# Gate projections moved from the joint input windows into the first mixers of pairs, other window bounds, a quarter-size last inversion level, and key norms from keys times keys

## The chip, the cores and the metric

The kernel runs on one NeuronCore of one Trainium2 chip. The time is the device time of one launch in microseconds (us).

## The reference, cut to what matters

One decoder layer on x of 1024 tokens by 1024 features, float32. Two mixers (retention and gated delta rule) share one input projection; then every token takes 8 x 16 experts out of 16384 by product keys, and each expert is a row of `peer_u` and a row of `peer_v`.

```python
h = _rmsnorm(x, ln1_w[l]); proj = (h @ w_in[l])
rq, rk, rv, rg, gq, gk, gv, gz, ga, gb = jnp.split(proj, offsets, axis=-1)
o_r = groupnorm(_retention(rope(rq), rope(rk), rv))
y_r = o_r * ret_norm_w[l] * jax.nn.silu(rg)
cq, ck, cv = split(silu(causal_conv(concat([gq, gk, gv]))))
q_g = cq * lax.rsqrt(jnp.sum(cq * cq, -1) + NORM_EPS)
k_g = ck * lax.rsqrt(jnp.sum(ck * ck, -1) + NORM_EPS)
o_g = _gated_delta_rule(q_g, k_g, cv, g_dec, beta)   # per chunk: m = I + strict(beta k k^T decay), a 128x128 triangular solve
y_g = _rmsnorm(o_g, gdn_norm_w[l]) * jax.nn.silu(gz)
x = x + concat([y_r, y_g]) @ w_out[l]
h2 = _rmsnorm(x, ln2_w[l])
# _peer: q = h2 @ wq; top-16 of each half; top-16 of the sums -> ids, gate
act = gelu(einsum('tkd,td->tk', u_tab[ids], h2))
x = x + einsum('tk,tkd->td', gate * act, v_tab[ids]); return _rmsnorm(x, lnf_w)
```

## The kernel before, in words

The 1024 tokens are eight chunks of 128. All engines run their own instruction lists, written out in Python and joined by semaphores.

**The expert stream.** Chunk n has 64 steps (PAIRS), 512 in all. A step is two gathers on GpSimd's queue (L452), each of 128 rows of 8 KB (u and v of one expert), 1.05 MB. VectorE takes the dot product of the u half with the token (L1161), ScalarE makes gelu and a diagonal tile (L841, L847), TensorE multiplies the diagonal by the v half into `y_ps` (L476). The ten `uv` buffers (RING) hold five steps: the gather of step s waits until TensorE has done step s-5 (`v_used`). Each engine has its own `upto(place)`, which deals it the steps up to that place between other work; TensorE deals step s-1 where the others deal s.

**Windows and mixers.** `window(n)` gives two places in the stream (numbers of steps). Inside window n, `route` of chunk n runs: the last two query products, scores, the top-16 on VectorE in groups of heads (`GROUPS`), which end in `ids` (L1519), and, if chunk n+1 is "alone" or "first", `inputs(n+1)`: norm, transposes, input projections. Between window n and window n+1 lies the mixer of chunk n+1 (`mix`), whose 34 marks (`turn`) are spread by the table PIECES. KIND is start, alone, then (first, second) three times: for a pair, `inputs` of the first chunk projects both chunks from the same weight block, one product for `actT` and one for `actT_ahead`. So windows 1, 3 and 5 hold joint projections of chunks (2, 3), (4, 5), (6, 7); windows 2, 4, 6, 7 hold none. I call mixers 2, 4, 6 first mixers, and 3, 5, 7 second mixers.

**Weights.** A projection of 512 columns (IN_NAMES: gk, gq, gv, rqk, rv, rg, gz) is two blocks of 1 MB. SyncE loads them one after the other (L410) into two buffers `wbuf`, each when the block two before it is used up (`consumed`). Per `inputs` there are 14 blocks, per chunk 4 for the output and 8 for the queries.

**Banks.** Everything else that TensorE makes goes round six PSUM banks in the order of the list `USES`; `take` waits until the use six before has been read.

**The inverse.** The mixer inverts the 128x128 matrix of each of 4 heads in levels T1, 1 to 6. Level i: P = NT x T, masked by VectorE into Pm, then Q = TT x Pm and R = Pm x TT, subtracted from T and TT (L709 to L716, L1361 to L1369). The norms of q and k come from squares (L993) and eight products with ones (L655); `kk` is made late, from k and k times beta (`kbT`, L1269), and NT is `kk` times the decay mask.

**The start.** Chunk 0 has no stream beside it; between its marks TensorE makes late products (`FILL`, L555). ScalarE issues four constant loads (L915) right after `hT`.

## Time and profile before

| what | value |
|---|---|
| median of three runs | 3143.29 us |
| lowest, highest | 3141.07, 3143.57 us |
| the profiled execution's own time | 3143.25 us |
| its span | 3141.3 us (1.95 us less) |
| busy: TensorE, VectorE, ScalarE, GpSimd | 76%, 66%, 37%, 37% |
| moved by DMA | 1265.78 MB, 403 GB/s over the span |

How to read it: no engine is busy all the time, and the DMA engines are. The profile gives the moved GB/s of each stretch; a stretch that falls below the rate of the others is one in which data were not asked for in time. Traces are cut here at the places where the windows begin and end (the dot product of that step on VectorE).

### The profile page before, as it was taken

What the parts mean: (1) busy time and instruction counts of PE and PEld (TensorE: products, weight loads), DVE (VectorE), ACT (ScalarE), POOL (GpSimd) and SP (SyncE); (2) the same over time, 40 slices, a digit from 0 to 9 for tenths busy, and PEclk for the clock granted to TensorE, in tenths of its full rate; (3) what the DMA queues carried; (4) which work ended last, traced back from release to release, by engine and by line L of the source; (5) the groups of instructions that cost most, each with busy time, mean ns of one, the idle gap of its engine ahead of it and who ended that gap; (6) DMA issues with size and microseconds to landing.
All of it is one profiled execution on the core that took longest, in us unless ns stands there. A gap on an engine that the chain in (4) does not pass through costs nothing.

```text
span 3141.3 us, 36341 instructions
## 1 busy us (share of the span) xinstructions
PE 2386.6 (76%) x12496; PEld 1389.6 (44%) x12496; DVE 2076.6 (66%) x5408; ACT 1173.6 (37%) x3421; POOL 1175.5 (37%) x1030
## 2 busy tenths in 40 slices
PE   8877787998874787997876587798787567765554
PEld 7753355764541345663552144575355124431111
DVE  4475855668579854667749874656856976486444
ACT  2233433344334432435323533424433343232222
POOL 0033533235333442334434443234443444344442
PEclk9998898998987898998998789899998689877777
DMA  8399999999999999999999999999999999999997
GB/s 344 141 405 420 417 411 401 396 409 419 420 415 400 419 420 420 386 418 419 419 420 415 420 419 416 390 405 420 419 420 420 420 419 418 419 402 418 420 420 319
DMA packets 177736, 1265.78 MB, mean 403 GB/s; under 512 B 21520, under 2 KB 21776, under 8 KB 25104
## 3 DMA queue, kind: packets, MB, share of 16 engines
q0 software_dynamic: 147456, 1073.81, 83.0%
q1 hardware_dynamic: 28368, 183.72, 14.2%
q10 hardware_dynamic: 1728, 5.94, 0.5%
q8 instruction: 99, 1.62, 0.2%
q14 instruction: 85, 0.70, 0.1%
HBM read 1259.19 MB, written 4.19 MB: 402 GB/s over the span
## 4 chain that ended last, share of the span: by engine, by line
DMA 36%; PE 36%; DVE 16%; ACT 6%; issue 3%; POOL 3%; SPq 0%; ACTq 0%; POOLq 0%; DVEq 0%
DMA uv<-uv_tab,ids 33%; PE y_ps L476 13%; PE bank L533 8%; DVE uv L1161 7%; PE bank L525 7%; PE bank L540 3%; POOL uv L452 3%; DMA wbuf<-w 2%; ACT diag L847 2%; PE y_ps L555 1%; DVE area L1221 1%; DVE area L1455 1%; PE bank L590 1%; DMA uv<-w 1%; ACT gelu L841 1%
## 5 line engine op out<-in xcount | busy, mean ns | idle before, releaser
L452 POOL DMA_INDIRECT uv<-uv_tab,ids x1024 | 1175.0, 1147 | 1933.0 <-PE y_ps L476 1589.8
L1161 DVE CUSTOM_DVE_ANT_0 uv<-uv,h 128x1024 f32<-128x1024 f32 x1024 | 1237.6, 1223 | 783.9 <-DMA uv<-uv_tab,ids 777.4
L476 PE MATMUL y_ps<-uv,diag 128*64 128x512 f32 x4096 | 1187.2, 712 | 515.2 <-ACT diag L847 494.1
L476 PEld LDWEIGHTS y_ps<-uv,diag 128*64 128x64 f32 x4096 | 289.1, 156 | 1168.5 <-ACT diag L847 687.4
L841 ACT ACTIVATE gelu<-dots 128x2 f32<-128x2 f32 x512 | 104.1, 203 | 1429.8 <-DVE dots L1161 1429.4
L533 PE MATMUL bank<-actT,wbuf 128*128 128x128 f32 x2688 | 343.0, 289 | 42.8 <-DMA wbuf<-w 37.8
L533 PEld LDWEIGHTS bank<-actT,wbuf 128*128 128x128 f32 x2688 | 329.6, 204 | 99.8 <-issue 72.4
L847 ACT ACTIVATE diag<-gated,gelu 128x64 f32<-128x64 f32 x1024 | 300.7, 340 | 66.9 <-PE y_ps L476 8.2
L837 ACT ACTIVATE gated<-smalls,gate 128x64 f32<-128x64 f32 x1024 | 293.9, 336 | 7.8 <-DVE acc L1175 7.8
L525 PE MATMUL bank<-wbuf,actT 128*128 128x256 f32 x960 | 226.8, 390 | 23.3 <-DMA wbuf<-w 21.5
L525 PEld LDWEIGHTS bank<-wbuf,actT 128*128 128x128 f32 x960 | 181.7, 194 | 91.7 <-issue 49.5
L540 PEld LDWEIGHTS bank<-arena 128*128 128x128 f32 x1208 | 150.6, 199 | 78.6 <-issue 57.2
L540 PE MATMUL bank<-arena 128*128 128x128 f32 x1208 | 167.2, 291 | 10.9 <-DVE arena L1361 9.0
L841 ACT ACT_TABLE_LOAD x90 | 115.5, 1283 | 1.6
L1455 DVE FIND_INDEX8 area<-area,arena 128x8 uint32<-128x128 f32 (+1 forms) x384 | 99.9, 279 | 0.0
L590 PE MATMUL bank<-keys_sb,arena 128*128 128x128 f32 x256 | 44.3, 327 | 69.5 <-ACT arena L869 68.5
L525 PE MATMUL bank<-wbuf,actT_ahead 128*128 128x256 f32 x384 | 89.1, 385 | 0.0
L1451 DVE MAX8 area<-arena 128x8 f32<-128x128 f32 (+1 forms) x384 | 79.8, 273 | 9.6 <-ACT arena L1081 4.6
L1221 DVE SCALAR_TENSOR_TENSOR area<-conv_in,conv_w,area 128x128 f32<-128x128 f32 x288 | 82.1, 347 | 2.5
L1161 DVE DVE_READ_ACCUMULATOR2_ANT dots<- 128x1 f32 x1024 | 83.7, 82 | 0.0
L525 PEld LDWEIGHTS bank<-wbuf,actT_ahead 128*128 128x128 f32 x384 | 71.1, 190 | 26.6 <-issue 17.8
L590 PEld LDWEIGHTS bank<-keys_sb,arena 128*128 128x128 f32 x256 | 37.6, 226 | 84.4 <-ACT arena L869 71.2
(221 smaller groups left out, 1874.2 us busy)
## 6 DMA issues: line engine op xcount, KB each, us to landing
wbuf<-w SPq DMA_DIRECT2D x146, 1024.0 KB, 9.5
uv<-w SPq DMA_DIRECT2D x20, 1024.0 KB, 23.9
uv<-uv_tab,ids POOLq DMA_INDIRECT x1024, 16.1
acc<-x SPq DMA_DIRECT2D x8, 512.0 KB, 12.8
y<-acc ACTq DMA_DIRECT2D x8, 512.0 KB, 7.6
rowbuf<-x SPq DMA_DIRECT2D x5, 512.0 KB, 12.6
actT_ahead<-x SPq DMA_DIRECT2D x3, 512.0 KB, 19.1
keys_sb<-keysT ACTq DMA_DIRECT2D x1, 1024.0 KB, 16.0
```

The source lines that it names most:

```text
L452: nc.gpsimd.indirect_dma_start(out=uv[i % RING][:, :, :].rearrange("p z d -> p (z d)"), out_offset=None, in_=uv_tab, in_offset=bass.Indire ...
L476: done = mm(y_ps[z][64 * j:64 * j + 64, :], diag[:, i % DIAGS, :], uv[i % RING][:, 1, 512 * z:512 * z + 512], start=(s % PAIRS == 0), stop ...
L525: last = mm(b[:, WB * half_:WB * half_ + WB], src[:, k, :], wb[:, k, :], start=(k == 0), stop=(k == KT - 1))
L533: last = mm(b[:, o:o + P], wb[:, k, P * i:P * i + P], src[:, k, :], start=(k == 0), stop=(k == KT - 1))
L540: last = mm(b[:, P * h:P * h + P], lhs[:, h, :], rhs[:, h, :], start=True, stop=True)
L590: last = mm(b[:, P * i:P * i + P], qT[:, t, :], keys_sb[:, t, :], start=True, stop=True)
L837: made = A(gated[:, step % 2, j, :], stack, ACT.Copy, scale=gate[n % 2][:, j, pair:pair + 1])
L841: A(gelu[:, step % 2, :], dots[:, d0:d0 + 2], ACT.Gelu).then_inc(S["gelu"], 1)
L847: made = A(diag[:, (2 * step + j) % DIAGS, :], gated[:, step % 2, j, :], ACT.Copy, scale=gelu[:, step % 2, j:j + 1])
L1161: V.tensor_tensor_reduce(out=u, in0=u, in1=h2[n % 2][:, j, :], scale=1.0, scalar=0.0, op0=ALU.mult, op1=ALU.add, accum_out=dots[:, i % DOT ...
L1221: last = V.scalar_tensor_tensor(dst, src, conv_w[:, i, j:j + 1], dst, ALU.mult, ALU.add)
L1455: last = V.max_index(index(t)[:, o:o + 8], vals(t)[:, o:o + 8], src(t))
```

## The change

Windows: joint ones become longer (34 steps instead of 30), the second mixers shorter. The four gate blocks (rg, gz) of a pair leave `inputs` and are made in the first mixer, eight matmuls at each of the marks 6 to 13, both chunks into halves of one bank. The last level makes only the one 64x64 quarter of P and R that is not zero, and no Q. `kk` comes early from k times k; its diagonal gives the squares for k's norm on VectorE (`kk_sums`); the beta row now multiplies the decay mask. At the start the four constant loads are issued later. Chunks 4, 6 and 7 get three groups of heads instead of two. What is computed is the same.

| window n | 1 | 2 | 3 | 4 | 5 | 6 | 7 |
|---|---|---|---|---|---|---|---|
| before | 55 to 83 | 118 to 138 | 176 to 206 | 244 to 264 | 304 to 334 | 372 to 392 | 436 to 456 |
| after | 55 to 82 | 119 to 140 | 172 to 206 | 246 to 267 | 300 to 334 | 374 to 395 | 438 to 458 |

```diff
-GROUPS = [[(0, 1), (1, 2), (2, 4), (4, PH)] if n == 0 else [(0, 2), (2, 4), (4, PH)] if n < 3 else [(0, 3), (3, PH)]
+GROUPS = [[(0, 1), (1, 2), (2, 4), (4, PH)] if n == 0 else [(0, 2), (2, 4), (4, PH)] if n in (1, 2, 4, 6, 7) else [(0, 3), (3, PH)]
...
-        for name, event in zip(LATE_NAMES, LATE_EVENTS):
+        for name, event in zip(LATE_NAMES[0:2 if kind == "first" else 4], LATE_EVENTS):
             uses += projection(name, event)
-    uses += own(("gc", "gc_in", 1, 0), ("gc_row", "E", 1, 0), ("ss", "norm_in", 1, 0),
-                ("kT", "kst", 1, 0), ("qk", "attn", 1, 0), ("beta_row", "kbT", 1, 0),
-                ("vT", "vb", 1, 0), ("kk", "NT", 1, 0),
-                ("T1", "inv_TT", LEVELS, 0))
+    uses += own(("gc", "gc_in", 1, 0), ("gc_row", "E", 1, 0), ("kk", "NT", 1, 0), ("ss", "norm_in", 1, 0),
+                ("kT", "kst", 1, 0), ("qk", "attn", 1, 0), ("beta_row", "NT", 1, 0),
+                ("vT", "vb", 1, 0), *gates("rg0"),
+                ("T1", "inv_TT", LEVELS, 0), *gates("rg1"))
     for i in range(1, LEVELS):
-        uses += level(i)
+        uses += level(i) + own(*gates({1: "gz0", 2: "gz1"}.get(i)))
...
+GATE_FILL = {mark: 8 for mark in range(6, 14)}
+GATED = [p + 0.75 * (i in GATE_FILL) for i, p in enumerate(PIECES)]
-WINDOW = {"first": (16, 14), "second": (12, 8), None: (12, 8)}
+WINDOW = {"first": (20, 14), "second": (10, 11), None: (10, 10)}
-        return ((-3, 22), (55, 83), (118, 138))[n]
+        return ((-3, 22), (55, 82), (119, 140))[n]
...
+            def gates_late(c):
+                n = c.n
+                for name in ("rg0", "rg1", "gz0", "gz1"):
+                    b = take(n, name)
+                    wb = weight_block()
+                    for a, src in enumerate((actT, actT_ahead)):
+                        for k in range(KT):
+                            last = mm(b[:, WB * a:WB * a + WB], src[:, k, :], wb[:, k, :], start=(k == 0), stop=(k == KT - 1))
+                            if k == KT - 1 and a:
+                                last.then_inc(gates_made, 1)
+                            yield
...
             def inputs(c, at):
-                names = IN_NAMES[0:3] if c.kind == "start" else IN_NAMES
+                names = IN_NAMES[0:{"start": 3, "first": 5}.get(c.kind, 7)]
-                at(0.22 if n < 2 else 0.26)
+                early = 0 if n < 2 else 7 / length(n - 1)
+                at(early or 0.22)
-                first = 0.25 if n < 2 else 0.29
+                first = 0.25 if n < 2 else 8 / length(n - 1)
-                products, done = 14 * len(projected), [0]
+                products, done = 2 * len(names) * len(projected), [0]
...
                 all_rows(n, "gc_row", T[:, :, :])
+                pe.wait_ge(*event("silu_conv", n, 0))
+                by_head(n, "kk", conv[:, 4:8, :], conv[:, 4:8, :])
-                for i in range(2 * H):
+                for i in range(H):
                     last = mm(b[:, i:i + 1], norms[:, i, :], ones[:, 0:1], start=True, stop=True)
...
-                pe.wait_ge(*event("kbT", n))
-                by_head(n, "kk", conv[:, 4:8, :], kbT)
...
+                    if i == LEVELS - 1:
+                        b = take(n, f"P{i}")
+                        for h in range(H):
+                            last = mm(b[64:128, P * h:P * h + 64], NT[0:64, h, 64:128], T[0:64, h, 0:64], start=True, stop=True)
...
+                        b = take(n, f"R{i}")
+                        for h in range(H):
+                            last = mm(b[0:64, P * h + 64:P * h + 128], Pm[64:128, h, 0:64], TT[64:128, h, 64:128],
+                                      start=True, stop=True)
+                        continue
...
-                at(0.20 if n < 2 else 0.24)
+                at(0.20 if n < 2 else 6.3 / length(n - 1))
...
                 if n == 0:
-                    for dst, src in ((ret_qdec[:, :, :], qdec), (smalls[:, :], small),
-                                     (keys_sb[:, :, :], keysT), (lnf_row[:, :], rows.partition_broadcast(P))):
-                        act.dma_start(dst, src).then_inc(late_in, 16)
...
                 if c.kind == "start":
+                    for dst, src in ((ret_qdec[:, :, :], qdec), (smalls[:, :], small),
+                                     (keys_sb[:, :, :], keysT), (lnf_row[:, :], rows.partition_broadcast(P))):
+                        act.dma_start(dst, src).then_inc(late_in, 16)
                     return
...
+                    if c.kind == "first" and i == 1:
+                        follows(act, "ret_mixed", n)
+                        gates_block("rg0", gate_r, "gR_half")
...
+                    b = filled(dve, "kk", c)
+                    for h in range(H):
+                        last = V.tensor_tensor_reduce(out=NT[:, h, :], in0=b[:, P * h:P * h + P], in1=ident, scale=1.0, scalar=0.0,
+                                                      op0=ALU.mult, op1=ALU.add, accum_out=st[:, 88 + h:89 + h])
+                    last.then_inc(S["kk_sums"], 1)
...
-                V.tensor_tensor(kbT[:, :, :], conv[:, 4:8, :], heads(filled(dve, "beta_row", c)), ALU.mult
-                                ).then_inc(S["kbT"], 1)
+                link(V.tensor_tensor(kbT[:, :, :], cmask[:, :, :], heads(filled(dve, "beta_row", c)), ALU.mult))
-                V.tensor_tensor(NT[:, :, :], heads(filled(dve, "kk", c)), cmask[:, :, :], ALU.mult).then_inc(S["NT"], 1)
+                V.tensor_tensor(NT[:, :, :], heads(filled(dve, "kk", c)), kbT[:, :, :], ALU.mult).then_inc(S["NT"], 1)
...
-                early = 0.22 if n > 0 else 0.37
+                early = 5.9 / length(n) if n > 0 else 0.37
```

What moves, at the places of which the prediction speaks. TensorE in window 3, from the replication of the tokens (L790, after L860) on: transposes (L500, after L537), the small products for a and b (L615, L666), the projections (L533, L570) and the stream's steps (L476, L513; x4 is one step). Before:

```order
L476 MATMUL y_ps<-uv,diag 64x512 x12
L500 MATMUL bank<-tab,rowbuf 128x128 x8
L500 MATMUL bank<-tab,actT_ahead 128x128 x8
L476 MATMUL y_ps<-uv,diag 64x512 x4
L615 MATMUL bank<-w_ab_sb,actT 128x8 x8
L615 MATMUL bank<-w_ab_sb,actT_ahead 128x8 x8
L533 MATMUL bank<-actT,wbuf 128x128 x16
L476 MATMUL y_ps<-uv,diag 64x512 x4
L533 MATMUL bank<-actT_ahead,wbuf 128x128 x16
L476 MATMUL y_ps<-uv,diag 64x512 x4
L533 MATMUL bank<-actT,wbuf 128x128 x16
L533 MATMUL bank<-actT_ahead,wbuf 128x128 x16
```

After:

```order
L513 MATMUL y_ps<-uv,diag 64x512 x8
L537 MATMUL bank<-tab,rowbuf 128x128 x8
L537 MATMUL bank<-tab,actT_ahead 128x128 x8
L513 MATMUL y_ps<-uv,diag 64x512 x4
L666 MATMUL bank<-w_ab_sb,actT 128x8 x8
L666 MATMUL bank<-w_ab_sb,actT_ahead 128x8 x8
L570 MATMUL bank<-actT,wbuf 128x128 x16
L513 MATMUL y_ps<-uv,diag 64x512 x8
L570 MATMUL bank<-actT_ahead,wbuf 128x128 x16
L513 MATMUL y_ps<-uv,diag 64x512 x4
L570 MATMUL bank<-actT,wbuf 128x128 x16
L513 MATMUL y_ps<-uv,diag 64x512 x4
```

One step fewer lies ahead of the transposes, two follow the first projection, and from there on one or two steps stand between two projections, where before there were one or none.

TensorE in mixer 2, from the last step ahead of T1 to level 2. Before:

```order
L476 MATMUL y_ps<-uv,diag 64x512 x12
L500 MATMUL bank<-tab,arena 128x128 x4
L476 MATMUL y_ps<-uv,diag 64x512 x8
L540 MATMUL bank<-arena 128x128 x4
L500 MATMUL bank<-tab,area 128x128 x4
L476 MATMUL y_ps<-uv,diag 64x512 x4
L540 MATMUL bank<-arena 128x128 x8
L476 MATMUL y_ps<-uv,diag 64x512 x4
L540 MATMUL bank<-arena 128x128 x4
```

After (L630 is half of a gate block, eight matmuls of one chunk):

```order
L513 MATMUL y_ps<-uv,diag 64x512 x8
L630 MATMUL bank<-wbuf,actT_ahead 128x256 x8
L537 MATMUL bank<-tab,arena 128x128 x4
L513 MATMUL y_ps<-uv,diag 64x512 x8
L630 MATMUL bank<-wbuf,actT 128x256 x8
L577 MATMUL bank<-arena 128x128 x4
L537 MATMUL bank<-tab,area 128x128 x4
L513 MATMUL y_ps<-uv,diag 64x512 x8
L630 MATMUL bank<-wbuf,actT_ahead 128x256 x8
L577 MATMUL bank<-arena 128x128 x8
L513 MATMUL y_ps<-uv,diag 64x512 x4
L630 MATMUL bank<-wbuf,actT 128x256 x8
```

The gate products stand between the levels, each behind one or two steps.

VectorE in the mixer of chunk 0, between the decay rows and the reciprocal of the norms. Before:

```order
L1246 TENSOR_TENSOR st<-bank,st 128x4
L1219 TENSOR_SCALAR area<-conv_in,conv_w 128x128 x4
L1221 SCALAR_TENSOR_TENSOR area<-conv_in,conv_w,area 128x128 x12
L1224 COPY conv_in<-conv_in 128x4x3
L1258 RECIPROCAL st<-st 128x8
```

After (L1341 is the new sum over the diagonal):

```order
L1341 ISA arena,st<-bank,tab 128x128
L1341 ISA st 128x1
L1341 ISA arena,st<-bank,tab 128x128
L1341 ISA st 128x1
L1341 ISA arena,st<-bank,tab 128x128
L1341 ISA st 128x1
L1341 ISA arena,st<-bank,tab 128x128
L1341 ISA st 128x1
L1311 TENSOR_SCALAR area<-conv_in,conv_w 128x128 x4
L1313 SCALAR_TENSOR_TENSOR area<-conv_in,conv_w,area 128x128 x12
L1316 COPY conv_in<-conv_in 128x4x3
L1355 RECIPROCAL st<-st 128x8
```

The third convolution now stands behind four sums that wait for `kk`.

## Rows read from the trace of the kernel before

**Rows 1.** The page: busy time, DMA rate by slice, table loads, gathers.
```profile
PE 2386.6 (76%) x12496; PEld 1389.6 (44%) x12496; DVE 2076.6 (66%) x5408; ACT 1173.6 (37%) x3421; POOL 1175.5 (37%) x1030
...
GB/s 344 141 405 420 417 411 401 396 409 419 420 415 400 419 420 420 386 418 419 419 420 415 420 419 416 390 405 420 419 420 420 420 419 418 419 402 418 420 420 319
...
L841 ACT ACT_TABLE_LOAD x90 | 115.5, 1283 | 1.6
...
uv<-uv_tab,ids POOLq DMA_INDIRECT x1024, 16.1
```

**Rows 2.** By stage: busy PE, PEld, DVE, ACT, POOL; clock, DMA share, GB/s.
```profile
0.00:142.40 142.40, 123.75 (x874) 114.18 (x875) 63.20 (x215) 40.16 (x79) 5.29 (x11) 0.98 0.60 233
...
302.30:485.70 183.40, 143.10 (x750) 81.36 (x746) 126.79 (x282) 80.86 (x231) 73.90 (x64) 0.89 1.01 415
485.70:680.30 194.60, 176.14 (x1075) 127.82 (x1074) 126.03 (x397) 74.54 (x207) 59.39 (x54) 0.93 0.98 398
680.30:884.20 203.90, 163.21 (x841) 93.77 (x840) 132.77 (x290) 85.28 (x243) 83.51 (x74) 0.91 1.01 420
884.20:1003.90 119.70, 74.91 (x384) 36.37 (x383) 106.83 (x364) 43.19 (x124) 46.99 (x41) 0.82 0.98 403
1003.90:1209.60 205.70, 157.72 (x804) 88.95 (x805) 139.18 (x301) 87.52 (x256) 86.91 (x76) 0.88 1.01 420
1209.60:1412.50 202.90, 181.48 (x1090) 129.20 (x1091) 126.88 (x377) 75.47 (x214) 66.39 (x57) 0.93 0.99 406
...
1964.20:2165.80 201.60, 182.14 (x1094) 129.97 (x1094) 126.81 (x376) 76.15 (x214) 65.97 (x56) 0.93 0.98 402
...
2739.40:2853.90 114.50, 78.31 (x379) 36.22 (x380) 101.62 (x335) 41.12 (x122) 47.65 (x39) 0.77 1.00 407
```

**Rows 3.** The same columns, stretches of 10 us in window 1, then window 5.
```profile
540.00:550.00 10.00, 6.39 (x24) 3.49 (x24) 9.68 (x41) 8.27 (x22) 6.20 (x6) 0.53 0.73 277
...
570.00:580.00 10.00, 10.00 (x79) 8.09 (x79) 9.00 (x33) 4.68 (x12) 2.10 (x2) 1.00 0.96 362
...
650.00:660.00 10.00, 10.00 (x46) 6.54 (x42) 6.51 (x10) 4.19 (x12) 4.63 (x4) 1.00 0.88 337
...
2030.00:2040.00 10.00, 10.00 (x54) 8.71 (x53) 8.76 (x28) 5.53 (x18) 0.40 (x1) 0.66 0.69 285
2040.00:2050.00 10.00, 10.00 (x79) 8.29 (x78) 7.93 (x38) 0.86 (x3) 4.66 (x4) 1.00 0.69 237
```

**Rows 4.** Timeline, TensorE, window 5: start, us, line, shape, count, [idle before].
```profile
2002.40 2.08 PE L590 MATMUL bank<-keys_sb,arena 128*128 128x128 f32 x8 [12.07 <-ACT arena L869]
...
2031.94 6.48 PE L533 MATMUL bank<-actT,wbuf 128*128 128x128 f32 x32
2038.34 1.94 PE L476 MATMUL y_ps<-uv,diag 128*64 128x512 f32 x8
...
2049.52 3.74 PE L533 MATMUL bank<-actT_ahead,wbuf 128*128 128x128 f32 x32
```

**Rows 5.** Waits of the whole span: total us, times, longest.
```profile
POOL uv L452 <- DVE ids L1519: 144.7, 2, 135.2
...
ACT gate_g L869 <- PE bank L525: 35.1, 6, 8.0
```

**Rows 6.** Timeline, TensorE in mixer 5: an output block, shaped as a gate block.
```profile
1901.95 3.72 PE L525 MATMUL bank<-wbuf,actT 128*128 128x256 f32 x16
```

**Rows 7.** Timeline of the start, and from the page the landing of the keys.
```profile
41.25 3.57 PE L655 MATMUL bank<-tab,area 128*128 128x1 f32 x16 [3.15 <-ACT area L993]
...
45.31 0.20 DVE L1258 RECIPROCAL st<-st 128x8 f32<-128x8 f32 x1 [1.47 <-ACT st L978]
...
58.91 0.41 DVE L1298 TENSOR_TENSOR area<-qk_r,ropes 128x256 f32<-128x256 f32 x1
...
93.50 1.95 PE L540 MATMUL bank<-arena 128*128 128x128 f32 x16
...
keys_sb<-keysT ACTq DMA_DIRECT2D x1, 1024.0 KB, 16.0
```

104 lines of the change are left out of this document (82 added, 22 removed).

## The prediction

> **What bounds the kernel now.** I read the page first [rows 1]: TensorE is busy 76% and VectorE 66% of the span, while the rate in most slices is 419 to 420 GB/s. The full rate is the bound, and the change removes no transfer, so a gain can only come from time in which the DMA engines are short of requests. I call that time lost: length x (1 - GB/s / 420). The table by stage [rows 2] says where it is. The start loses 142.4 x (1 - 233/420) = 63.4 us. The windows with joint projections, 1, 3 and 5, lose 10.2, 6.8 and 8.6 us, 25.6 together. Windows 2 and 7 lose 4.8 and 3.5, mixer 1 loses 2.2, mixers 2 and 3 nothing.
>
> In windows 3 and 5 TensorE is busy 181.5 of 202.9 us and 182.1 of 201.6. But it isn't short of time evenly. The cut into 10 us [rows 3] shows 285 and 237 GB/s at 2030 to 2050: 3.2 + 4.4 = 7.6 of the 8.6 us of window 5. The timeline there [rows 4] tells why. TensorE waits 12.07 us for ScalarE's copy of the queries; then come replication, transposes, the small products, and a first projection of 6.48 us in a stretch whose granted clock is 0.66, between the levels of 1.2 and 2.4 GHz; at 1.00 a step takes 1.94 us and a projection 3.74. The ring holds 5 steps x 5.0 us (2 x 1.05 MB at 420 GB/s) = 25 us, of which a gather needs 16.1 to land [rows 1]: some 9 us are left for everything else, and this burst is longer. In window 1 the same burst comes after a stretch at 277 GB/s (3.4 us lost) [rows 3]: GpSimd waited for the ids, once at the start (135.2 us) and once for 144.7 - 135.2 = 9.5 us [rows 5]. Window 1 then stays short: 362 and 337 GB/s long after the burst [rows 3].
>
> **The change part by part.**
>
> *Pace of the joint projections.* One product of one chunk and one block takes 3.74 us [rows 4], call it 3.8. Before, windows 3 and 5 hold 28 of them in 0.71 x 30 = 21.3 steps: 1.31 x 3.8 + 1.94 = 6.9 us of TensorE per step. DMA needs 5.0 + 14/21.3 x 2.5 (a block of 1.05 MB) = 6.6. After, 20 in 26 steps: 0.77 x 3.8 + 1.94 = 4.9 against 5.0 + 10/26 x 2.5 = 6.0. Window 1: 7.3 against 6.8 before, and after, with 20 in 19 steps, 5.9 against 6.3. So TensorE is under DMA everywhere after the burst, with little room in window 1.
>
> *The burst.* By the order of the instructions the transposes come one step earlier after the replication (two steps ahead instead of three), so one step is held behind the first projection that was not, and its gather comes up to 10 us later. The steps after it come 3 to 6 us earlier, since no two projections stand together any more. I take 7.6 us down to about 5. The norm of x also no longer waits for VectorE's next step: the reciprocals stand 7.5 steps into the window in both, but the window has begun 4 steps sooner.
>
> Windows 3 and 5 together: from 15.4 to 9.4, **-6 us**. Bounds: all of it gone, -15; the burst 1 us worse each and nothing behind it to win, +2. Window 1: its ids come half a step earlier (62 instead of 62.5 dealt), which is worth 1 of the 3.4 us, and what lies behind the burst goes: 10.2 to 5.2, **-5 us** (bounds -9, 0).
>
> *Gate blocks in the first mixers.* Four blocks for two chunks are 8 x 3.72 us [rows 6] = 29.8 us of TensorE. Mixer 2 grows by 2 steps: TensorE 163.2 + 29.8 + 2 x 1.94 = 197 us, in 203.9 + 2 x 5.0 + 4 x 2.5 = 224 us: 88%, where the joint windows that lose are at 90%. The cover is TensorE's idle time between levels; its order puts a step ahead of each piece, and behind it the product P or Q of the level, for which VectorE waits up to 3.7/2 + 1.94 us longer. VectorE has 65% there. The two blocks for gz are loaded 3 marks ahead of their use, about 4 steps or 20 us. I take +0.5 us for each of three, **+1.5** (bounds -0.5 and +9; the upper is 3 us a mixer, what the burst costs a window of the same load).
>
> *Shorter second mixers.* Mixer 3 goes from 38 to 32 steps: 205.7 - 30 = 176 us for TensorE's 157.7 - 6 x 1.94 = 146 and VectorE's 139.2 - 6 x 2.6 = 124. The nearest row is mixer 1, 33 steps in 183.4 us, which loses 2.2 [rows 2]. Mixer 5 is alike (33 steps), mixer 7 hardly changes. **+1.5** (0 to +4).
>
> *Windows 2, 4, 6, 7.* 20 or 21 steps as before. The first group of two heads is ready 0.25 x 21 = 5.25 steps into a window that opens 2 steps later, where 3 heads were ready at 7.5: the same place within half a step. A third group adds some 5 us of VectorE: window 2, which has three, takes 106.8 us, window 7 with two 101.6 [rows 2]. Their losses, 4.8 and 3.5, show no order by groups. **0** (-3 to +4).
>
> *Last level and norms.* Away from the start they are hidden under DMA. At the start nothing hides them: TensorE is busy 123.8 of 142.4 us. Q and R of a level take 1.95 us [rows 7], P half of that; four products of 64 columns instead of 128 halve P and R, and Q goes: 2.9 to 1.0, -1.9 us. Eight products with ones go from the 3.57 us [rows 7], but `kk` and the sum stand in their place. VectorE reaches the reciprocal (45.31) only after the third convolution: about 3 us later; it waits 1.47 us there and about 2.5 us more behind it until T1, so I book +0.5. The four constant loads (1.7 MB, 4 us at full rate) leave the stretch of the first weight blocks; 4 us is the most that can give, and with TensorE busy for all but 18.6 us of the start I take 1.0. They are first needed at 58.91 [rows 7]; issued some 2 us ahead of the products with ones (41.25), with 16.0 us to land [rows 7], they are there at 55, if the last of the four isn't slower. Start: **-2.4** (-4 to +3).
>
> A rule of the Trainium skill bears on the last level: by "TensorE: Matmul & The Clock Gate" (Part 2: What happens when you issue a matmul) a product takes as many cycles as columns stream in, however few rows it has. A quarter of the area then costs half the time; by area it would be a quarter, and the start 0.5 us better. No row of before has a product of 64 columns.
>
> ScalarE gets 13 more table loads, 16.7 us at 1.283 us each [rows 1]; it is busy 37% of the span, and the row shows 1.6 us of idle time ahead of 90 loads. "ScalarE: Activation LUTs" of the Trainium skill (What ACT_TABLE_LOAD costs) adds a drain of 1.38 us to each, 35 us in all; no row here shows it, and the sum would not change.
>
> **The sum.** 3143.25 us, the profiled execution's own time (span 3141.3 and 1.95 around it, 0.04 below the median): -2.4 - 5 - 6 + 1.5 + 1.5 + 0 = -10.4, so **3133 us**.
>
> **The rivals.**
>
> *The burst is the whole loss.* Pace is not the cause; only what lies behind the bursts goes, about 2 us a window (in window 5: 8.6 - 7.6 = 1.0, in window 1 some 3). Then -2.4 - 6 + 3 = -5.4: 3138 us. For it: 7.6 of 8.6 us lie in 20 us. Against: the order behind the first projection changes too.
>
> *All joint loss goes.* The earlier norm and the slower pace lift both: -2.4 - 25.6 + 1 = -27: 3116 us. For it: a demand well under DMA's. Against: the 12.07 us wait and the half clock stay.
>
> *Slower: ScalarE is held by the gate blocks.* In its fixed order ScalarE waits for TensorE's product before it goes on with gelu and diagonals. Such waits were 35.1 us in 6, 5.9 each [rows 5]. The first mixers get 12. A wait costs nothing while the 9 us of the ring hold; beyond them, with VectorE's chain waiting for P in the same marks, each costs about 1.5 us: +18, and with the other terms 3133 - 1.5 + 18 = 3150 us. For it: TensorE at 88%. Against: mixer 2 lost nothing with ScalarE at 42%.
>
> *The start goes the wrong way.* Constants late, convolution in the path: +3 instead of -2.4: 3138 us.
>
> **How the numbers follow.** The forecast has 0.42, the burst alone 0.24, all gone 0.12, slower 0.14, the start 0.08. A measurement of this kernel tells 0.2%, 6.3 us, from no change: faster is below 3137.0. The forecast with its spread gives 0.38 of its 0.42 to faster, all gone 0.12, the burst case 0.07, the start 0.02: 0.59. Slower: the gate case 0.12 and 0.01 of the others, 0.13. Same: 0.28. The range from 3118 to 3147 leaves out most of the slower case and half of all gone, 0.2 together.
>
> **What would show it.** Each step right: windows 1, 3, 5 lose 5, 4 and 5 us; first mixers stay at 419 GB/s or more with TensorE near 88%; mixers 3 and 5 lose under 2.5 us; the first dot product comes near 140 us instead of 142.4. Wrong: a stretch under 400 GB/s in a first mixer with ScalarE waiting for the gate product; a gather queue that waits for ids in windows 2, 4, 6, 7; windows 3 and 5 with their 7 us unchanged behind the replication; VectorE waiting near 59 us for the constants.

## The result, and the profile after

| | before | changed |
|---|---|---|
| median | 3143.43 us | 3100.44 us |
| lowest, highest | 3141.07, 3148.46 us | 3098.10, 3102.39 us |
| span of the profiled execution | 3141.3 us | 3096.1 us |

The ratio is 0.9861 (95% interval 0.9849 to 0.9873): 43 us less. I had predicted 3133 us with a range of 3118 to 3147. The direction held, the size didn't, and most of the gain came from something that the prediction doesn't contain.

The page of the changed kernel, first the busy times, then GB/s in 40 equal slices, then table loads (count, us, mean ns, idle time before them):

```profile
PE 2330.2 (75%) x12368; PEld 1355.8 (44%) x12368; DVE 2082.0 (67%) x5551; ACT 1188.0 (38%) x3449; POOL 1187.9 (38%) x1030
...
GB/s 349 143 408 426 427 427 403 404 426 423 416 420 424 412 412 421 414 426 418 426 426 409 424 420 426 394 426 427 427 423 415 418 427 426 427 399 419 427 427 340
DMA packets 177736, 1265.77 MB, mean 409 GB/s; under 512 B 21520, under 2 KB 21776, under 8 KB 25104
...
L911 ACT ACT_TABLE_LOAD x97 | 124.5, 1283 | 1.7
```

The busy shares are within one point of [rows 1], and the bytes are the same. What differs is the rate in the best slices: 426 to 427 GB/s, where it was 419 to 420. It differs even in the last part, after all windows, where both kernels run the same instructions. Columns as in [rows 2], the kernel before first:

```profile
2900.00:3100.00 200.00, 111.20 (x318) 24.12 (x316) 97.79 (x159) 50.69 (x200) 89.48 (x80) 0.77 1.01 420
```
```profile
2850.00:3050.00 200.00, 114.86 (x328) 25.27 (x326) 100.58 (x163) 51.94 (x205) 91.58 (x82) 0.76 1.01 427
```

The order of the work there is the same in both, so a new order can hardly be the cause. The trace's records of single packets (a packet here is one row of 8 KB) agree: on the gathers' queue they took 313 ns in the median and 320 at the 90th percentile before, 309 and 309 after. 1265.8 MB at 420 GB/s are 3014 us, at 427 they are 2964, so 49 us could come from the rate alone. Measured against its own full rate the changed kernel is short of requests for 3096.1 - 2964.4 = 131.7 us, the kernel before for 3141.3 - 3013.8 = 127.5.

The stages of the changed kernel: start; window 1; mixer 2; window 2; mixer 3; window 3; mixer 4; windows 4 and 5; mixer 6; windows 6 and 7.

```profile
0.00:140.40 140.40, 122.86 (x859) 112.23 (x860) 62.85 (x222) 39.76 (x79) 5.36 (x11) 0.98 0.61 237
...
478.30:657.70 179.40, 157.07 (x989) 110.36 (x989) 123.68 (x393) 66.98 (x195) 64.28 (x54) 0.93 0.98 407
657.70:868.50 210.80, 165.80 (x846) 98.52 (x843) 135.94 (x305) 94.47 (x262) 84.90 (x72) 0.92 1.01 421
868.50:994.80 126.30, 81.59 (x448) 42.07 (x447) 109.19 (x367) 45.95 (x130) 52.93 (x44) 0.84 1.01 421
994.80:1166.30 171.50, 130.19 (x646) 71.33 (x646) 123.40 (x284) 76.39 (x222) 74.33 (x60) 0.86 1.00 414
1166.30:1383.00 216.70, 184.16 (x1132) 126.04 (x1134) 136.29 (x393) 76.12 (x230) 81.08 (x72) 0.95 1.01 420
1383.00:1608.00 225.00, 179.16 (x895) 105.94 (x892) 142.49 (x316) 99.67 (x278) 91.95 (x78) 0.91 1.01 423
1608.00:1735.50 127.50, 80.26 (x426) 37.60 (x424) 109.03 (x368) 45.87 (x130) 51.82 (x46) 0.83 1.00 416
...
1910.70:2125.70 215.00, 184.19 (x1096) 123.00 (x1095) 136.23 (x392) 74.16 (x227) 81.53 (x72) 0.92 0.99 415
2125.70:2354.90 229.20, 183.12 (x937) 107.23 (x938) 142.99 (x317) 102.22 (x285) 93.87 (x81) 0.92 1.01 425
2354.90:2478.30 123.40, 74.72 (x383) 33.66 (x381) 108.80 (x367) 44.52 (x128) 49.29 (x43) 0.81 1.00 415
...
2707.10:2826.90 119.80, 78.56 (x382) 38.25 (x384) 106.82 (x364) 44.49 (x127) 48.62 (x40) 0.77 0.98 404
```

What could make every packet faster? The diff shown above leaves out one line, which I took for bookkeeping: four columns for the new sums of squares.

```diff
-        st = sb("st", [88])
+        st = sb("st", [92])
```

Tensors lie behind one another in SBUF in steps of 32 bytes, so a row of `st` takes 384 bytes where it took 352. `st` stands ahead of the ring `uv`, so every ring buffer moved by 32 bytes: `uv0` began at byte 124384 of a partition, 224 above a multiple of 256, and now begins at 124416 = 486 x 256. That is theory A. Its rival, theory B: the new order of work lets the transfers run faster.

### The profile page after: what moved, and what is told of

It is laid out like the page before. It is cut to its first block, busy times and chain, and to the rows that moved or that the text cites. A ratio compares the mean times of both kernels' runs of the same rounds, so it can differ in the third digit from the quotient of the medians.

```text
span 3096.1 us, 36299 instructions
## 1 busy us (share of the span) xinstructions
PE 2330.2 (75%) x12368; PEld 1355.8 (44%) x12368; DVE 2082.0 (67%) x5551; ACT 1188.0 (38%) x3449; POOL 1187.9 (38%) x1030
## 4 chain that ended last, share of the span: by engine, by line
PE 33%; DMA 30%; DVE 24%; ACT 7%; issue 4%; POOL 2%; ACTq 0%; POOLq 0%; DVEq 0%; SPq 0%
DMA uv<-uv_tab,ids 24%; PE y_ps L513 12%; DVE uv L1253 11%; PE bank L570 7%; DMA wbuf<-w 6%; PE bank L562 4%; PE bank L630 3%; PE bank L577 2%; DVE area L1313 2%; POOL uv L489 2%; ACT diag L917 2%; DVE area L1558 1%; PE bank L537 1%; ACT actT L945 1%; PE y_ps L592 1%
## 5 line engine op out<-in xcount | busy, mean ns | idle before, releaser
L489 POOL DMA_INDIRECT uv<-uv_tab,ids x1024 | 1187.4, 1160 | 1877.7 <-PE y_ps L513 1534.2
L513 PE MATMUL y_ps<-uv,diag 128*64 128x512 f32 x4096 | 1158.2, 698 | 525.4 <-ACT diag L917 474.1
L513 PEld LDWEIGHTS y_ps<-uv,diag 128*64 128x64 f32 x4096 | 288.3, 153 | 1168.8 <-ACT diag L917 676.1
L570 PE MATMUL bank<-actT,wbuf 128*128 128x128 f32 x2688 | 337.7, 287 | 48.4 <-DMA wbuf<-w 39.8
L570 PEld LDWEIGHTS bank<-actT,wbuf 128*128 128x128 f32 x2688 | 323.3, 200 | 106.8 <-issue 72.2
L907 ACT ACTIVATE gated<-smalls,gate 128x64 f32<-128x64 f32 x1024 | 294.2, 336 | 13.6 <-DVE acc L1267 13.6
L562 PE MATMUL bank<-wbuf,actT 128*128 128x256 f32 x768 | 188.6, 401 | 36.4 <-DMA wbuf<-w 22.5
L562 PEld LDWEIGHTS bank<-wbuf,actT 128*128 128x128 f32 x768 | 149.3, 199 | 95.1 <-issue 40.5
L577 PEld LDWEIGHTS bank<-arena 128*128 128x128 f32 x1016 | 122.3, 192 | 51.2 <-issue 39.7
L577 PE MATMUL bank<-arena 128*128 128x128 f32 x1016 | 133.8, 281 | 4.6 <-DVE arena L1462 2.9
L570 PEld LDWEIGHTS bank<-actT_ahead,wbuf 128*128 128x128 f32 x576 | 65.7, 192 | 15.4 <-issue 15.4
L570 PE MATMUL bank<-actT_ahead,wbuf 128*128 128x128 f32 x576 | 69.1, 278 | 0.0
L1505 DVE TENSOR_TENSOR acc<-bank,acc 128x512 f32<-128x512 f32 x14 | 9.7, 691 | 82.9 <-PE bank L562 82.9
## 6 DMA issues: line engine op xcount, KB each, us to landing
rowbuf<-x SPq DMA_DIRECT2D x5, 512.0 KB, 12.2
keys_sb<-keysT ACTq DMA_DIRECT2D x1, 1024.0 KB, 13.6
```

The lines of the kernel that those rows point to most:

```text
L489: nc.gpsimd.indirect_dma_start(out=uv[i % RING][:, :, :].rearrange("p z d -> p (z d)"), out_offset=None, in_=uv_tab, in_offset=bass.Indire ...
L513: done = mm(y_ps[z][64 * j:64 * j + 64, :], diag[:, i % DIAGS, :], uv[i % RING][:, 1, 512 * z:512 * z + 512], start=(s % PAIRS == 0), stop ...
L562: last = mm(b[:, WB * half_:WB * half_ + WB], src[:, k, :], wb[:, k, :], start=(k == 0), stop=(k == KT - 1))
L570: last = mm(b[:, o:o + P], wb[:, k, P * i:P * i + P], src[:, k, :], start=(k == 0), stop=(k == KT - 1))
L577: last = mm(b[:, P * h:P * h + P], lhs[:, h, :], rhs[:, h, :], start=True, stop=True)
L907: made = A(gated[:, step % 2, j, :], stack, ACT.Copy, scale=gate[n % 2][:, j, pair:pair + 1])
```

## Experiments: the address of the ring

**The kernel before, its ring moved by 32 bytes.** Theories A and B are furthest apart here, since no instruction changes.

```diff
+        pad = sb("pad", [8])
         uv = [sb(f"uv{i}", [2, D]) for i in range(RING)]
```

> The kernel before, unchanged but for 32 unused bytes in front of the ring, which the change also puts there (st grows from 88 to 92 columns, and tensors are laid out in steps of 32 bytes). The first byte of uv0 in a partition goes from 124384 (224 above a multiple of 256) to 124416 (a multiple of 256). No instruction changes. Theory A, the address: packets of 8 KB take 309 ns at the 90th percentile instead of 320, full slices show 427 GB/s instead of 420, and 1265.8 MB / 420 - 1265.8 / 427, some 45 us at most, go: 3095 to 3105 us. Theory B, the order of the work makes the faster rate: 3143 us and 420 GB/s as before. Both in part: between, 3120, and the rate between.

Measured: 3100.49 us, ratio 0.9855 (0.9838 to 0.9871). The slices:

```profile
GB/s 348 143 396 426 427 422 408 402 407 426 426 407 411 427 426 426 387 424 426 426 427 416 427 426 427 405 390 426 427 427 423 426 420 426 427 418 415 427 427 336
```

Thirty-two unused bytes give the whole 43 us, with no instruction changed. Theory B falls as the explanation of the rate.

**The changed kernel, its ring put back to 224.** The same edit with `[56]`.

> The changed kernel with 224 unused bytes in front of the ring, so that uv0 begins at 124640, 224 above a multiple of 256, as in the kernel before. No instruction changes. What is left against the kernel before is then the change of the order alone. Theory A: 420 GB/s again, and between 3133 us (the sum that I predicted for the order) and 3143 us (the order is worth nothing). Theory B: 3100 us and 427 GB/s as without the bytes.

Measured: 3138.79 us, ratio 0.9982 (0.9973 to 0.9992). The slices are those of [rows 1] again:

```profile
GB/s 354 144 404 420 420 420 399 406 420 418 417 409 420 416 406 407 414 420 420 419 420 400 419 420 416 381 420 420 419 418 407 412 420 419 420 386 414 420 420 333
```

So the order alone, which is what I had predicted, is worth 0.18%, 5.5 us (2.5 to 8.5).

**Is it the ring?** The first run also moved what lies behind the ring, the ids among it. Here the pad stands behind the ring.

```diff
         uv = [sb(f"uv{i}", [2, D]) for i in range(RING)]
+        pad = sb("pad", [8])
```

> The kernel before with 32 unused bytes behind the ring instead of in front of it: the ring stays where it was (224 above a multiple of 256), but the two buffers h2, the ids that the gathers read, the gates, dots and diagonals move by 32 bytes, as they also did in the run that was as fast as the changed kernel. Theory A, the ring's own address: 3143 us, 420 GB/s. Rival, the address of the ids (or of another tensor behind the ring) makes the transfers faster: 3100 us, 427 GB/s.

Measured: 3143.11 us, ratio 0.9997 (0.9987 to 1.0006). Moving what lies behind the ring does nothing, so it is the ring's own address.

**A multiple of what?** Three more places, with `[32]`, `[16]` and `[8]` in front of the ring of the changed kernel.

> The changed kernel with 128 unused bytes in front of the ring: uv0 128 above a multiple of 256, yet on a multiple of 64 and of 128. If A holds, this tells what the address must be a multiple of. A1, 64 or 128 bytes are enough: 3100 us, 427 GB/s, as on 256. A2, each row of 8 KB takes a 33rd piece whenever it doesn't start on 256: the time of the kernel with uv0 at 224. A3, the cost goes by the 32 byte words that are read or written besides: 8 + 31 x 8 + 4 = 260 here against 263 at 224 and 256 at 0, so 4/7 of the loss: some 3120 us. Theory B: 3100 us. The Trainium skill, DMA: Bandwidth & Descriptors (How a descriptor splits into AXI transactions), describes pieces of 256 bytes that start on multiples of 256; A2 and A3 are two readings of it, and no run has yet shown either.

> The changed kernel with its ring 64 above a multiple of 256, where the weight buffers stand. So far 0 gives 3100 us, 128 gives 3130 and 224 gives 3139. A2, any place off 256 costs a 33rd piece per row: 3130 to 3139. A3, the words of 32 bytes decide (258 against 256, 2/7 of the loss of 224): 3111 us. A4, 64 costs nothing, as the weight buffers suggest, whose packets take 309 ns at 64 in the changed kernel, and whose move to 256 brought nothing: 3100.

> The changed kernel with its ring 32 above a multiple of 256. A2: 3130 to 3139 us. A3 (257 words against 256, 1/7 of the loss): 3106. A5, what counts is a multiple of 64 and besides it the distance from 256: as slow as 224, 3139.

| ring above a multiple of 256 | median | ratio to before | best slices | median 8 KB packet |
|---|---|---|---|---|
| 0 (the changed kernel) | 3100.44 us | 0.9861 | 427 GB/s | 309 ns |
| 128 | 3130.08 | 0.9949 (0.9932 to 0.9966) | 421, 422 | 312 |
| 64 | 3131.57 | 0.9964 (0.9953 to 0.9975) | 421 | 312 |
| 224 | 3138.79 | 0.9982 (0.9973 to 0.9992) | 420 | 313 |
| 32 | 3140.86 | 0.9995 (0.9986 to 1.0004) | 420 | 313 |

A1 falls, and so does A4 (64 costs about 31 us). A3, a cost by 32-byte words, falls hardest: it gave 3106 us for 32, and 32 is the slowest. A2 holds in its first part: any place off 256 costs some 30 us. A place that isn't a multiple of 64 costs about 9 us more (128 to 224 on one chip 8.7, 64 to 32 on another 9.3). A5 had that, and its 3139 us for 32 came out; 64 and 128 are alike, so nothing here shows that the distance from 256 counts. Why it is so, no run shows. The rule of the Trainium skill, "DMA: Bandwidth & Descriptors" (How a descriptor splits into AXI transactions), that pieces of 256 bytes start on multiples of 256, agrees with the first part: off 256 is slower. As an estimate from that rule, a 33rd piece would be 3%; the mean packet goes from 312.3 ns to at most 317.0, 1.5%. The count of 32-byte words that the expected text takes from the same section (A3) puts the four places in the order 32, 64, 128, 224; the measured order is another, and the measurement decides.

**The weight buffers.** If the address counts for every transfer, the weight blocks have 15% of the effect to give. (Both edits in one; the comments give the numbers of the second.)

```diff
+        pad_w = sb("pad_w", [48])   # [56] in the second
         wbuf = [sb(f"wbuf{i}", [KT, WB]) for i in range(2)]
...
+        pad = sb("pad", [16])       # [8] in the second
         uv = [sb(f"uv{i}", [2, D]) for i in range(RING)]
```

> The changed kernel with the two weight buffers on a multiple of 256 too (192 unused bytes in front of them, 64 in front of the ring, which stays on one). The weight blocks are 26 of 1.05 MB for every pass over them, about 15% of all bytes. If A holds and goes for weight blocks as for rows of the ring: their packets of 8 KB (313 ns in the mean, 0 queue aside) come down by up to 5 ns, and 15% x 45 = 7 us go: 3093 us. If the excess at 64 above a multiple of 256 is small (A3: 258 words against 256) about 2 us: 3098. Theory B, or none of it for weights: 3100.

> The changed kernel with its two weight buffers 32 above a multiple of 256 instead of 64, the ring on 256. A ring at 32 cost 40 us for 85% of the bytes. If the address counts for weight blocks as it does for rows of the ring, they cost 15/85 x 40 = 7 us here (and 5 of them were there to win at 64, which the run with both on 256 didn't show): 3102 to 3107 us. If it doesn't count for them: 3100.

Measured: 3101.16 us with the weights on 256 (ratio 0.9855, 0.9837 to 0.9873), 3100.98 us with them at 32 (0.9868, 0.9847 to 0.9889), beside 3096.59 us for the changed kernel on the chip of the latter (0.9855, 0.9832 to 0.9877). The times can't tell 0 from 5 us. The packets tell more: on the queue of the weight blocks an 8 KB packet takes 309 ns in the median and at the 90th percentile with the weight buffers at 0, 32 and 64. In the kernel before, where they stand at the same 64, it is 311 and 319. So what slows these copies is not the address of `wbuf`.

Nor is the difference one between gathers and plain copies. At the start SyncE copies weight blocks into the ring itself:

```profile
uv<-w SPq DMA_DIRECT2D x20, 1024.0 KB, 17.8
```

In the first 60 us, long before the first gather (issued at 134.35 us; 136.42 in the kernel before), most 8 KB packets on SyncE's queue belong to these copies. With the ring on a multiple of 256 the packets of that stretch take 309 ns in the median and at the 90th percentile, in all eleven traces. With the ring off it they take 312 or 313, and 319 or 320 at the 90th percentile, in all six. A plain copy pays for the ring's address as a gather does, and with no gather beside it. Why `wbuf` at 32 or 64 doesn't pay stays open: while the ring was off 256, `wbuf` was always at 64.

## Experiments: the order

All of these have their ring on a multiple of 256.

**What the order is worth at the faster rate.**

> The kernel before with its ring on a multiple of 256, this time on the same chip as the changed kernel. On different chips they came out alike (3100.5 and 3100.4 us), while with the ring off 256 the changed order is 5.5 us faster. If the order is worth the same in both places: this kernel 5 us above the changed one. If the third group and the fuller first mixers cost more at the faster rate, whose steps are 4.9 us instead of 5.0: within 2 us of it.

> The changed kernel itself, to stand on the same chip beside the kernel before with its ring on 256: 3100 us, and 5 us or 0 us below that one.

Measured on one chip: 3102.13 us for the old order (ratio 0.9866, 0.9845 to 0.9887) and 3096.59 us for the new (0.9855, 0.9832 to 0.9877). That is 5.5 us by the medians, 3.5 by the ratios, and the intervals overlap. The pair before it (3100.49 and 3100.44) shows no difference. The two together put the order at 0 to 5 us, and a gain isn't shown: each ratio is uncertain by 4 to 7 us.

**The small parts alone**: the old order of projections, windows and groups, with the quarter level, the norms and the late constants.

```diff
-GATE_FILL = {mark: 8 for mark in range(6, 14)}
+GATE_FILL = {}
...
-WINDOW = {"first": (20, 14), "second": (10, 11), None: (10, 10)}
+WINDOW = {"first": (16, 14), "second": (12, 8), None: (12, 8)}
...
-        return ((-3, 22), (55, 82), (119, 140))[n]
+        return ((-3, 22), (55, 83), (118, 138))[n]
```

> The kernel before with its ring on a multiple of 256 (3100.5 us) and only the small parts of the change: the last level as a quarter, the keys' norms from keys times keys, and the four constant loads issued late. Projections, windows and groups are those of before. By my recorded step on the start: -2.4 us (-4 to +3), all of it ahead of the first dot product, which comes near 140 us instead of 142.2, and nothing after it: 3098 us. If the quarter and the norms also free time on the bound of the mixers, up to 1 us in each of seven: 3091 to 3094. If the late constants are in the path: VectorE waits near 59 us, 3103.

Measured: 3097.78 us (ratio 0.9854, 0.9839 to 0.9869) against 3100.49 and 3102.13: 3 to 4 us less. The size fits the prediction's -2.4, but with intervals of 5 us either side the time alone doesn't show it. The traces do better: the first dot product comes at 141.1 us here and at 139.2 to 141.2 in the twelve traces of the changed order, against 141.6 to 143.5 in the four with the old start.

**Two groups instead of three** in windows 4, 6 and 7.

```diff
-... else [(0, 2), (2, 4), (4, PH)] if n in (1, 2, 4, 6, 7) else [(0, 3), (3, PH)]
+... else [(0, 2), (2, 4), (4, PH)] if n < 3 else [(0, 3), (3, PH)]
```

> The changed kernel (3100.4 us) with the groups of heads of the kernel before: windows 4, 6 and 7 route in two groups, heads 0 to 2 and then the rest, instead of three. Everything else is as changed, the ring stays on a multiple of 256. In the changed kernel VectorE is busy 109.0, 108.8 and 106.8 us of these windows against 101.7, 101.4 and 101.6 before, and the windows lose 3.2, 3.6 and 6.4 us against the full rate of 427 GB/s. Theory C, the third group's 5 to 7 us of VectorE are on the path there, since VectorE is busy 97 to 99% of most stretches of 10 us: the loss returns to that of the order before (0.7 to 2.3 us each), 6 to 8 us go: 3093 us. Rival, the window now opens two steps later, so three heads are ready 10 us later and the gather queue waits for the ids that the kernel before had only 2 to 4 us early: 5 to 8 us more in each of three windows, less what C gives: 3105 to 3115 us, with waits of GpSimd for the ids in all three. Nothing of both: 3100.

Measured: 3091.22 us (ratio 0.9841, 0.9823 to 0.9858). Windows 4, 6 and 7 of this run:

```profile
1607.60:1731.50 123.90, 83.44 (x435) 39.78 (x435) 103.93 (x339) 43.31 (x127) 51.95 (x46) 0.82 1.01 423
2348.00:2470.80 122.80, 77.76 (x397) 36.84 (x397) 104.00 (x339) 42.81 (x126) 51.17 (x43) 0.81 1.01 424
2701.60:2814.50 112.90, 73.33 (x380) 34.98 (x382) 101.47 (x334) 41.56 (x124) 45.53 (x39) 0.83 0.99 409
```

VectorE is busy 5 us less in each, and they lose 1.2 + 0.9 + 4.8 = 6.9 us against 427 GB/s instead of 3.3 + 3.5 + 6.5 = 13.3. The rival's waits for the ids are there too, one of 4.3 to 5.4 us in each of the three windows. Timeline of GpSimd, start and length in us, in brackets the idle time before it; then the total of these waits in this kernel, and in the changed one:

```profile
1659.22 0.94 POOL L489 DMA_INDIRECT uv<-uv_tab,ids  x1 [4.25 <-DVE ids L1622]
...
2397.99 0.94 POOL L489 DMA_INDIRECT uv<-uv_tab,ids  x1 [4.26 <-DVE ids L1622]
...
2747.70 0.94 POOL L489 DMA_INDIRECT uv<-uv_tab,ids  x1 [5.40 <-DVE ids L1622]
...
  DVE ids L1622: 155.9, 5
```
```profile
POOL uv L489 <- DVE ids L1622: 140.7, 2, 133.1
```

Waits and gain stand together: windows 4 and 6 run at 423 and 424 GB/s in spite of them, so the wait that I had named as a sign of trouble costs next to nothing there. In window 7 it may cost. Around and behind the wait at 2747.70 the rate falls to 390 and 373 GB/s (2740 to 2760 and 2760 to 2780 us), and window 7 loses 4.6 to 4.7 us in the two traces with two groups and late ids, 2.1 to 3.6 in the six with two groups and early ids.

**Two groups and the old places** of windows 2, 4, 6 and 7.

```diff
-WINDOW = {"first": (20, 14), "second": (10, 11), None: (10, 10)}
+WINDOW = {"first": (20, 14), "second": (12, 8), None: (12, 8)}
...
-        return ((-3, 22), (55, 82), (119, 140))[n]
+        return ((-3, 22), (55, 82), (118, 138))[n]
```

> As the run with two groups, and windows 2, 4, 6 and 7 also stand where they stood before (20 steps, opening 12 ahead of a chunk's last step instead of 10); gate blocks stay in the first mixers, windows 3 and 5 stay at 34 steps. Theory C: windows 4, 6, 7 lose 1 to 2 us each as in the kernel before with its ring on 256. Second mixers 3 and 5 begin 3 steps sooner and end 2 sooner, and keep what they lose. 3093 us. Rival of the run with two groups (ids late): here the ids are early again, so this run and not that one shows the gain: 3093 here and 3105 to 3115 there.

Measured: 3095.67 us (ratio 0.9842, 0.9825 to 0.9859). By the ratio it is the same as the run before it, and the ids are early again (2 waits). The times alone don't show that the third group was the cost: the changed kernel's interval (0.9849 to 0.9873) overlaps both. The traces do. Windows 4, 6 and 7 together lose 3.7 to 7.6 us in the eight traces with two groups (6.3 to 7.6 in the three of them with the new order of projections, at the new places or the old) and 12.2 to 15.0 us in the nine with three, wherever the ring stood; the table below has all of them. Neither the ids nor the places separate these two sets.

**Joint windows of 30 steps**, gate blocks still in the first mixers.

```diff
-WINDOW = {"first": (20, 14), "second": (10, 11), None: (10, 10)}
+WINDOW = {"first": (16, 14), "second": (10, 11), None: (10, 10)}
```

> The changed kernel with windows 3 and 5 of 30 steps as before instead of 34; they still hold 20 joint products, since the gate blocks stay in the first mixers. The windows open 4 steps later. Theory D, the burst is all: what lies behind the replication of x is the same burst, and 20 products in 22 steps are 0.91 x 3.8 + 1.94 = 5.4 us of TensorE per step against 4.9 + 10/22 x 2.46 = 6.0 of DMA, so nothing is lost elsewhere: 3100 us, windows 3 and 5 lose 3 to 6 us as now. Rival, the length of the windows is what lowered their loss (7.9 to 3.5 and 10.7 to 6.1 us at 427 GB/s): it returns, +4 us each, 3108 us.

Measured: 3097.18 us (ratio 0.9846, 0.9828 to 0.9863), no slower than the changed kernel. Window 2, mixer 3 and windows 3 and 5 of this run:

```profile
869.50:1003.00 133.50, 88.30 (x472) 46.98 (x472) 108.82 (x368) 46.09 (x130) 47.74 (x45) 0.81 0.97 403
1003.00:1198.00 195.00, 147.82 (x765) 83.31 (x766) 133.85 (x301) 84.29 (x245) 84.88 (x72) 0.90 1.01 426
1198.00:1387.90 189.90, 167.50 (x1015) 115.33 (x1015) 126.57 (x376) 69.27 (x208) 68.85 (x60) 0.93 0.99 413
1938.30:2129.60 191.30, 165.40 (x1032) 112.70 (x1030) 126.68 (x376) 69.98 (x209) 72.58 (x62) 0.95 1.00 417
```

Windows 3 and 5 lose 6.2 + 4.5 = 10.7 us here and 3.6 + 6.0 = 9.6 in the changed kernel. A loss that comes back with the old length doesn't show. These rows hold a warning too: window 2 loses 7.5 us and mixer 3 0.5 here, 1.8 and 5.2 in the changed kernel. The sum is about 7 to 8 in both; only the cut between them moved.

**Both together**, two groups and 30 steps.

> The changed kernel with both edits that the runs found free or better: two groups of heads in windows 4, 6 and 7 (3091 us alone) and windows 3 and 5 of 30 steps (3097 alone, against 3100). If the length of the joint windows is worth nothing, as their sum of losses says (10.3 against 9.6 us, and 7.5 us in window 2 and 0.3 in mixer 3 against 1.8 and 5.5): 3091 us. If the two gains add: 3088. If the first mixers, now 4 steps longer ahead of the window, and the groups stand in each other's way: 3097.

Measured: 3088.11 us (3085.39 to 3091.28), ratio 0.9828 (0.9815 to 0.9842). It is the fastest of all: 12 us below the changed kernel by the medians, 10 by the ratios. The part that the 30 steps add to the two groups (3 us) is inside the intervals.

## Why the prediction was wrong, step by step

**The step that failed: "The full rate is the bound, and the change removes no transfer, so a gain can only come from time in which the DMA engines are short of requests."** The first half held. The second took 420 GB/s for a property of the chip. It was one of this kernel's layout, and 32 bytes changed it to 427: 3143 to 3100 us with no instruction moved. The sum has no term for a change of the rate. The row was there [rows 1], but nothing in it says whether 420 is a ceiling, and I didn't ask what the change does to addresses. A diff that changes a tensor's size moves everything behind it.

**The order.** With the ring back at 224 the premise holds and my sum can be tried: 3138.8 us measured, 3133 predicted, -5.5 us for -10.4. It lies within the range, at about half the forecast gain and at the figure of the first rival; that it comes so near is in part luck. Windows 4, 6 and 7 went past their bound, and stretches that the sum doesn't have, mixer 1 and the one behind window 7, lose 1.5 and 2.8 us less. The rows of that run, in the order start, window 1, mixer 2, mixer 3, window 3, windows 4, 5, 6 and 7:

```profile
0.00:139.50 139.50, 121.73 (x862) 110.77 (x862) 62.87 (x223) 39.85 (x79) 5.42 (x12) 0.99 0.61 239
481.80:662.50 180.70, 157.76 (x996) 109.98 (x996) 123.72 (x394) 67.86 (x196) 64.55 (x55) 0.94 0.99 405
662.50:874.40 211.90, 168.05 (x833) 99.48 (x830) 136.21 (x305) 94.88 (x262) 86.41 (x72) 0.90 1.01 418
1003.70:1179.00 175.30, 132.16 (x682) 74.04 (x684) 123.62 (x285) 76.89 (x222) 73.09 (x62) 0.89 1.00 412
1179.00:1394.10 215.10, 183.65 (x1094) 123.45 (x1090) 136.57 (x392) 75.02 (x226) 75.28 (x69) 0.91 1.00 413
...
1626.50:1751.80 125.30, 74.31 (x390) 33.96 (x388) 108.92 (x368) 45.28 (x129) 51.83 (x44) 0.81 0.99 408
1931.70:2150.00 218.30, 183.10 (x1080) 120.95 (x1079) 136.27 (x392) 74.95 (x229) 77.27 (x71) 0.91 0.98 406
2384.30:2507.50 123.20, 79.67 (x383) 37.24 (x382) 108.53 (x368) 44.48 (x128) 52.06 (x43) 0.80 1.00 407
2742.30:2862.30 120.00, 77.46 (x384) 37.10 (x384) 106.73 (x364) 44.15 (x126) 49.18 (x41) 0.80 0.97 394
```

| term | predicted | measured there, loss against 420 GB/s |
|---|---|---|
| start | -2.4 | 142.4 to 139.5 us: -2.9 |
| window 1 | -5 | 10.2 to 6.5: -3.7 |
| windows 3 and 5 | -6 | 15.4 to 3.6 + 7.3 = 10.9: -4.5 |
| first mixers | +1.5 | mixer 2 from 0 to 1.0; at 427 GB/s larger, below |
| second mixers | +1.5 | mixer 3 from 0 to 3.3, but window 2 from 4.8 to 1.9 |
| windows 4, 6, 7 | 0 (at most +4) | 4.9 to 3.6 + 3.8 + 7.4 = 14.8: +9.9; the stretch behind window 7 loses 2.8 less |

(4.9 is from the kernel before: windows 4 and 6 at 416 and 419 GB/s in 116.2 and 115.2 us, window 7 in [rows 2].)

One pair of traces is thin for terms of 3 us: window 1 loses 10.1 us in the kernel before and 7.1 in the run that only moved what lies behind the ring. So here are all 17 traces, cut at the steps where their windows begin and end; losses are against 427 GB/s with the ring on a multiple of 256, 421.5 with it at 64 or 128, 420 with it at 32 or 224. "Old order" is that of projections and windows; the small parts alone count there, but for the start. Rates are not rounded here, so sums differ by up to half a us from those above.

| us | old order: median (lowest, highest) | changed order |
|---|---|---|
| length of the start | 142.3 (141.6, 143.5), 4 traces | 139.5 (139.2, 141.2), 13 |
| window 1, loss | 10.2 (7.1, 12.8), 5 | 7.6 (6.3, 11.7), 12 |
| windows 3 and 5 | 15.9 (15.2, 20.4), 5 | 11.0 (5.7, 17.0), 12 |
| mixers 2, 4, 6 | 0.7 (0.3, 1.6), 5 | 4.9 (1.7, 7.7), 12 |
| | two groups | three groups |
| windows 4, 6, 7 | 5.8 (3.7, 7.6), 8 | 14.1 (12.2, 15.0), 9 |

The start, the first mixers and the third group stand clear of the scatter. Windows 1, 3 and 5 went the forecast way, but their ranges overlap.

*The start* was right in size. The reciprocal came at 47.47 us instead of 45.31, 2.2 us later where about 3 was booked; the keys, issued at 37.05, landed 13.6 us later, and the first use of the constants was at 57.90: no wait near 59. Timeline and page:

```profile
37.05 0.45 ACTq L1012 DMA_DIRECT2D keys_sb<-keysT  x1
...
47.47 0.20 DVE L1355 RECIPROCAL st<-st 128x8 f32<-128x8 f32 x1
...
57.90 0.41 DVE L1394 TENSOR_TENSOR area<-qk_r,ropes 128x256 f32<-128x256 f32 x1
...
89.97 0.68 PE L767 MATMUL bank<-arena 64*64 64x64 f32 x8
...
keys_sb<-keysT ACTq DMA_DIRECT2D x1, 1024.0 KB, 13.6
```

The quarter product of four heads (eight instructions) takes 0.68 us. The full one of eight instructions took 1.05 us in the kernel before, at 84.75 and 90.88 us of its timeline. The rule of the Trainium skill that I quoted ("TensorE: Matmul & The Clock Gate", Part 2: What happens when you issue a matmul) would make it half, the area a quarter; it is 0.65. The rule is nearer, but something doesn't shrink with the columns.

*The joint windows* went the way I said, to three quarters of the size (-8.2 us for -11), and the mechanism is half confirmed. The burst behind the replication is still there in window 5 of the changed kernel (columns as before):

```profile
1970.00:1980.00 10.00, 10.00 (x53) 8.06 (x52) 8.37 (x20) 5.67 (x24) 2.88 (x2) 0.67 1.01 424
1980.00:1990.00 10.00, 10.00 (x67) 7.36 (x66) 6.39 (x9) 5.07 (x13) 3.89 (x4) 0.92 0.59 221
1990.00:2000.00 10.00, 10.00 (x71) 7.00 (x70) 5.05 (x15) 2.03 (x8) 4.01 (x5) 1.00 0.98 392
```

It costs 4.8 + 0.8 us where it cost 7.6, again with a granted clock of 0.67 just ahead of it. I had said 5. The runs with 30 steps add what I didn't know. At 30 steps, ring on a multiple of 256, windows 3 and 5 lose 15.9 to 20.4 us with 28 products (three traces) and 10.3 and 11.1 with 20 (two). So it is the products taken out, with the order of the projections that came with them, and not the windows' length. Which of those two it is wasn't tried, nor 28 products in 34 steps.

*The third group* is the term that failed within the order. I had its work right, "some 5 us of VectorE", and priced it at nothing, because windows 2 and 7 "show no order by groups". Two windows with different work around them are no evidence. VectorE is busy 109.0 of 127.5 us in window 4 of the changed kernel. From 1650 to 1730 us it is busy 93%, and the window's loss lies almost whole in three slices where it is full: 1.5 + 0.8 + 0.8 of 3.3 us. TensorE is full only in the first (columns as before):

```profile
1650.00:1660.00 10.00, 9.77 (x92) 5.18 (x88) 9.86 (x44) 5.74 (x16) 5.21 (x5) 0.98 0.95 365
1660.00:1670.00 10.00, 3.87 (x16) 0.97 (x16) 9.39 (x37) 2.47 (x10) 8.17 (x7) 1.00 0.98 393
...
1690.00:1700.00 10.00, 3.76 (x12) 0.90 (x14) 9.93 (x46) 2.79 (x11) 4.22 (x5) 0.83 1.00 393
```

A window like that has no cover for 5 us more. Taking the group away gave 9 us by the medians, 4 to 6 by the ratios (0.9861 or 0.9855 to 0.9841). Of the 10 us between the two profiled executions 6.6 lie in these three windows and 4 in windows 3 and 5, whose groups the edit doesn't touch; so the 9 is too much.

*Gate blocks.* The term was +1.5 with +9 as the upper bound. In the changed kernel mixers 2, 4 and 6 lose 3.0 + 2.1 + 1.1 us at 427 GB/s, against 0.7 in all for the old order with its ring on 256 (426 to 427 GB/s in each). That is +5.5, and +4 by the medians of the table. The bound was right and the value low. Nor does ScalarE look like the cause. It waited for gate products in 9 places, in all 27.6 us, at most 5.0 at once:

```profile
ACT gate_r L1048 <- PE bank L630: 12.5, 3, 5.0
...
ACT gate_g L1048 <- PE bank L630: 7.9, 3, 3.7
...
ACT L1048 <- PE bank L630: 7.2, 3, 2.8
```

In the kernel before it was twice that, since the 35.1 us of [rows 5] are those for `gate_g` alone. The row that the prediction left out:

```profile
ACT gate_r L869 <- PE bank L525: 20.6, 5, 10.1
```

Yet the one low slice of mixer 4 stands ahead of ScalarE's first gate block (1456.37 us), where TensorE has no idle time:

```profile
1440.00:1450.00 10.00, 10.00 (x49) 5.23 (x46) 4.96 (x13) 1.59 (x7) 5.96 (x6) 1.00 0.94 358
```

That fits the start of the gate pieces on TensorE; it is read from the trace and not tested.

*Table loads*: 13 more were expected, and the trace holds 226 for 213, 290.0 us for 273.3. The idle time ahead of the largest group of them stays at 1.7 us for 97, so the drain of 1.38 us of the Trainium skill's "ScalarE: Activation LUTs" (What ACT_TABLE_LOAD costs) doesn't show here either. Behind a load there is none: one that begins at 1420.32 us and takes 1.28 is followed by its ACTIVATE at 1421.61.

*The rivals.* "All joint loss goes" (3116) is nearest to 3100 in number and wrong in kind: windows 1, 3 and 5 still lose 8.4 + 3.6 + 6.0 us. The slower case needed ScalarE's waits to decide; they came and didn't. The sign I had named for trouble in windows 4, 6 and 7, gathers that wait for ids, appeared in a kernel that was no slower (3091 us).

## What to carry to other kernels

Before a prediction takes the best rate in a profile for a ceiling, look at the address of what is written: put buffers that take a stream of long rows on multiples of 256 bytes, and read every change of a tensor's size as a move of all that lies behind it. When the time moves by more than the changed stages hold, compare a stretch where both kernels run the same code; if the rate differs there, the cause isn't the order. And price extra work on an engine by how full that engine is in that very window, not by its mean.

## What the hardware showed that I hadn't expected

- The stream of 8 KB rows into this ring runs at 427 GB/s if its buffers begin on a multiple of 256 bytes, at 421 to 422 from 64 or 128 above one, at 420 from 32 or 224: 309, 312 and 313 ns a packet. It is worth 30 to 40 us of 3100. "SBUF — State Buffer" of the Trainium skill (Operand start alignment) asks only for a multiple of the element's size, and calls that a matter of legality, not of speed. All places tried here are legal by it, and they differ by up to 40 us.
- Plain copies into the same ring, before any gather runs, take 309 ns on a multiple of 256 and 312 or 313 off it. Copies into the two weight buffers take 309 ns from 0, 32 and 64 above a multiple of 256 alike, as long as the ring is on one.
- 1.7% more rate gave 1.4% less time. The start, 142 us at 232 or 233 GB/s, stayed as long, and the time short of requests rose from 127.5 to 3099.1 - 2964.4 = 134.7 us with the old order. Of these 7 us 1.5 are the start, whose bytes now count as less time; for the rest each step has 0.1 us less in which to hide its work, which fits but wasn't tried.
